# Expert rows weighted at copy-out and summed by accumulating gathers, in a four-layer block on one core

## The reference, cut to what matters

```
logits = x @ w_router                       # 8 experts
top_v, top_i = top_k(logits, 2)
gates = one_hot(top_i) * softmax(top_v)
out = sum over e of gates[:, e] * (silu(x @ w_gate[e]) * (x @ w_up[e])) @ w_down[e]
x = layer_norm(alpha * x + out, g, b)
x = x + (p @ w_ple_proj) * sigmoid(x @ w_ple_gate)
```

## Time and profile before

| what | us |
|---|---|
| median of three runs | 2200.12 (2200.06 to 2201.48) |
| the profiled execution: time | 2201.47 |
| the profiled execution: span | 2199.7 |
| PE busy | 2164.4 |
| DVE busy | 1724.8 |
| ACT busy | 1416.0 |
| POOL busy | 61.7 |

### The profile page before, as it was taken

One profiled execution on the slowest core, in us unless ns is written; L12 is line 12 of the kernel. 1 busy time (PEld: TensorE's weight loads), 2 busy tenths in 40 slices (PEclk: granted clock), 3 DMA queues, 4 the chain that ended last, 5 costly groups with the idle time before them and its releaser, 6 DMA issues.

```text
span 2199.7 us, 30807 instructions
## 1 busy us (share of the span) xinstructions
PE 2164.4 (98%) x11360; PEld 1806.4 (82%) x11360; DVE 1724.8 (78%) x1976; ACT 1416.0 (64%) x1582; POOL 61.7 (3%) x96
## 2 busy tenths in 40 slices
PE   8999999999999999999999999999999999999998
PEld 6788897778888888888888887779978898988888
DVE  6766556688898888888888889767668886776887
ACT  6644444767777777777777777656566556565554
POOL 3000000020000000000000003000000000000000
PEclk9999999999999999999999999999999999999999
DMA  9755554369999999999999999843135554224451
GB/s 390 273 185 190 192 190 175 120 256 397 358 397 368 390 374 384 378 382 380 371 388 376 389 365 403 323 177 130 68 145 190 184 200 148 86 106 157 188 189 61
DMA packets 83523, 573.26 MB, mean 261 GB/s; under 512 B 9744, under 2 KB 10368, under 8 KB 18224
## 3 DMA queue, kind: packets, MB, share of 16 engines
q1 hardware_dynamic: 77760, 545.29, 65.0%
q0 software_dynamic: 5376, 26.12, 3.2%
q10 hardware_dynamic: 288, 0.52, 0.1%
HBM read 564.03 MB, written 17.83 MB: 265 GB/s over the span
## 4 chain that ended last, share of the span: by engine, by line
PE 87%; DVE 6%; ACT 4%; issue 2%; DMA 1%; SPq 0%; POOL 0%; DVEq 0%; ACTq 0%; POOLq 0%
PE bank L829 64%; PE bank L897 10%; PE bank L899 5%; DVE w_lo L540 1%; ACT w_hi L535 1%; PE bank L1188 1%; DVE arena L2411 1%; PE bank L1316 1%; PE bank L1326 1%; ACT arena L1533 1%; DMA raw<-in_wu_qkv 1%; PE bank L952 0%; DVE arena L2091 0%; PE bank L944 0%; PE bank L798 0%
## 5 line engine op out<-in xcount | busy, mean ns | idle before, releaser
L540 DVE TENSOR_TENSOR w_lo<-raw,w_hi 128x2048 fp32r<-128x2048 f32 x505 | 1156.1, 2300 | 249.4 <-ACT w_hi L535 247.7
L535 ACT CAST w_hi<-raw 128x2048 fp32r<-128x2048 f32 x505 | 964.4, 1912 | 357.5 <-PE bank L829 275.1
L829 PE MATMUL bank<-w_hi,xT 128*128 128x512 f32 x2368 | 751.5, 392 | 6.4 <-DVE w_lo L540 3.3
L829 PEld LDWEIGHTS bank<-w_hi,xT 128*128 128x128 f32 x2368 | 444.6, 188 | 107.6 <-issue 7.0
L829 PE MATMUL bank<-w_lo,xT 128*128 128x512 f32 x1184 | 461.0, 389 | 0.0
L829 PE MATMUL bank<-w_hi,aT_hi 128*128 128x512 f32 x864 | 344.4, 399 | 1.0 <-DVE w_lo L540 1.0
L897 PE MATMUL bank<-xT,w_hi 128*128 128x512 f32 x960 | 339.9, 398 | 1.2 <-DVE xT L2035 0.6
L829 PE MATMUL bank<-w_hi,aT_lo 128*128 128x512 f32 x864 | 337.3, 390 | 0.0
L829 PE MATMUL bank<-w_lo,aT_hi 128*128 128x512 f32 x864 | 336.7, 390 | 0.0
L899 PE MATMUL bank<-xT,w_lo 128*128 128x256 f32 x960 | 269.3, 281 | 0.0
L829 PEld LDWEIGHTS bank<-w_lo,xT 128*128 128x128 f32 x1184 | 222.5, 188 | 44.7 <-issue 0.5
(11 more groups left out here) (348 smaller groups left out, 1689.2 us busy)
## 6 DMA issues: line engine op xcount, KB each, us to landing
raw<-in_wu_eg SPq DMA_DIRECT2D x112, 1024.0 KB, 7.3
raw<-in_wu_eu SPq DMA_DIRECT2D x112, 1024.0 KB, 7.2
raw<-in_wu_ed SPq DMA_DIRECT2D x112, 1024.0 KB, 7.2
raw<-in_wu_up SPq DMA_DIRECT2D x44, 1024.0 KB, 4.8
raw<-in_wu_ffn_gu SPq DMA_DIRECT2D x28, 1024.0 KB, 4.8
raw<-in_wu_in SPq DMA_DIRECT2D x28, 1024.0 KB, 4.8
raw<-in_wu_down SPq DMA_DIRECT2D x22, 1024.0 KB, 4.8
raw<-in_wu_ffn_d SPq DMA_DIRECT2D x14, 1024.0 KB, 4.8
```

The costliest lines, as they stand in the source:

```text
L535: nc.scalar.copy(w_hi[:, place(i), :], src).then_inc(*E.hi.mark("unit", i))
L540: nc.vector.tensor_tensor(w_lo[:, place(i), :], raw[:, i % RAW, :], w_hi[:, place(i), :].bitcast(F32), ALU.subtract) \
L829: mm = nc.tensor.matmul(o, l[i], r[j], start=(first and n == 0), stop=(last and n == 2), skip_group_check=not lone)
```

## The change

1. **Weights at copy-out.** Each expert row is scaled when ACT copies it out of its bank. For this DVE computes for each token the slot of its weight, POOL scatters the 512 weights into a DRAM table (four indirect DMAs of one float per partition) and loads it back as `w_slot`; in each turn DVE copies one column to `w_now`, and ACT's copy becomes an activation with a per-partition scale, behind one more wait.
2. **Accumulating gathers.** POOL's product and sum are gone. After the seventh expert's rows are stored, four indirect DMAs with an adding write go straight into R: both tiles for the first choice, then both for the second, each behind its tile's first one. Tokens of the eighth expert are pointed at row 0, which holds zeros.
3. **The eighth expert by a product.** Its rows are never stored. A 0/1 matrix of its members is made ahead of the loop (two DVE compares, two PE transposes, an ACT copy), and behind the loop four float32 matmuls `back x ye` put its rows in token order into banks 0 to 3, from which DVE's `take_rows` adds them. SP no longer waits for gathers.
4. **The branch.** PE's skip over the overflow loop becomes an explicit branch with a prefetch hint that is marked at the top of each turn.
5. **Orders.** One half of the second embedding pair runs behind the transposes of tile 0 in place of two idle products of 256 columns; the zeroing of `ye` moves from DVE (just ahead of the loop) to POOL (behind the norm of the mixer); `rows_and_gates` has fewer dependent steps.
6. **Room.** A constant `which` of 8 columns is added, and the constants' buffer is rounded up from 898 to 928 columns.

```
@@ -239,7 +240,7 @@
-        cst = sb("cst", [P, NC])
+        cst = sb("cst", [P, -(-NC // 32) * 32])
@@ sync: overflow_loads and the unit loads @@
-                    sp.wait_ge(*M.free[1].at("moe", "ye", 1))
-                    sp.dma_start(yg[NE * S:NE * S + P, :], moe["ye"]).then_inc(*M.put.mark("last"))
                     overflow_loads()
-                    for t in range(NT):
-                        sp.wait_ge(*high_in[t].at(t))
@@ gpsimd @@
+            def weights():
+                gp.wait_ge(*y_rows_ready.at())
+                for k, w in enumerate((w1, w2)):
+                    for t in range(NT):
+                        gp.indirect_dma_start(wg, bass.IndirectOffsetOnAxis(ap=w_rows[:, 2 * t + k:2 * t + k + 1], axis=0),
+                                              w[:, t:t + 1], None).then_inc(*wg_put.mark("all"))
+                gp.wait_ge(*wg_put.at("all"))
+                gp.dma_start(moe["w_slot"], wg.rearrange("(h r e) o -> r h (e o)", r=P, e=NE)).then_inc(*w_in.mark())
             def collect():
...
-                for t in range(NT):
-                    fetch(0, t, low_in)
-                gp.wait_ge(*low_in.last())
                 gp.wait_ge(*M.act.at("scaled"))
-                for t in range(NT):
-                    y = moe["y"][:, 0, t, :]
-                    nc.gpsimd.tensor_scalar(y, y, wlo[:, t:t + 1], None, ALU.mult).then_inc(*low_scaled.mark(t))
-                for t in range(NT):
-                    gp.wait_ge(*low_scaled.at(t))
-                    nc.gpsimd.tensor_tensor(R[:, t, :], R[:, t, :], moe["y"][:, 0, t, :], ALU.add).then_inc(*low_added.mark(t))
-                gp.wait_ge(*M.put.at("last"))
-                for t in range(NT):
-                    fetch(1, t, high_in[t])
+                for k in range(2):
+                    for t in range(NT):
+                        if k:
+                            gp.wait_ge(*rows_in[t].at(0))
+                        gp.indirect_dma_start(R[:, t, :], None, yg,
+                                              bass.IndirectOffsetOnAxis(ap=y_rows[:, 2 * t + k:2 * t + k + 1], axis=0),
+                                              compute_op=ALU.add).then_inc(*rows_in[t].mark(k))
+            gp.wait_ge(*x_ready.at(1, "mix", 1))
+            nc.gpsimd.memset(moe["ye"], 0.0).then_inc(*zeroed.mark())
             dispatch()
+            weights()
@@ tensor @@
+            def last_rows():
+                pe.wait_ge(*M.free[1].at("last", "members"))
+                for t in range(NT):
+                    for nb in range(2):
+                        pe.wait_ge(*M.free[nb].at("moe", "ye", nb))
+                        o = open_bank(M, 2 * t + nb)
+                        nc.tensor.matmul(o[:, :], moe["back"][:, t, :], moe["ye"][:, nb * 512:(nb + 1) * 512], start=True, stop=True) \
+                            .then_inc(*M.groups.mark("last", "rows", t, nb))
                 embeddings(L, 0)
                 if L:
-                    embeddings(L, 1)
-                    idle_products(3, 512, 512)
+                    embeddings(L, 1, (0,))
+                    idle_products(0, 512, 512)
                 turn_tile(stage, 0, ready, half=(lambda t: x_half.at(L, "ffn", t)) if L else None)
-                if L == 0:
-                    embeddings(L, 1)
-                else:
-                    idle_products(3, 256, 256)
+                embeddings(L, 1, (1,) if L else range(NT))
...
-                    idle_products(7, 512, 512)
+                    idle_products(7, 512)
+                    last_members()
+                    idle_products(7, 512)
...
                     with pe.Fori(0, NE) as e:
+                        overflow_skip = pe.mark_branch_hint_location()
                         with ev.loop(e):
                             experts(M, "moe", expert_base)
-                    with pe.If(r > 0):
+                    pe.br_lt(r, 1, on_true="pe_past_overflow", on_false="pe_overflow").branch_hint(overflow_skip)
+                    with nc.body("pe_overflow", valid_engines=[mybir.EngineType.PE]):
...
+                    nc.switch_bb("pe_past_overflow")
+                    last_rows()
@@ scalar @@
+                ac.wait_ge(*E.dve.at(tag, "weight"))
                 for h in range(2):
-                    nc.scalar.copy(moe["ye"][:, h * 512:(h + 1) * 512], bank[h][:, :]).then_inc(*E.free[h].mark(tag, "ye", h))
+                    nc.scalar.activation(results[E][:, h * 512:(h + 1) * 512], bank[h][:, :], ACT.Identity, scale=w_now[:, 0:1]) \
+                        .then_inc(*E.free[h].mark(tag, "ye", h))
...
+                    ac.wait_ge(*M.groups.at("last", "members"))
+                    nc.scalar.copy(moe["back"].rearrange("p t n -> p (t n)"), bank[1][:, 0:NT * P]) \
+                        .then_inc(*M.free[1].mark("last", "members"))
@@ vector @@
+                    if f == 1:
+                        ve.wait_ge(*w_in.at())
+                        ve.wait_ge(*turn_before(E.free[1], tag, "ye", 1))
+                        step(V_.tensor_copy(w_now, moe["w_slot"][:, tile:tile + 1, e]), E, tag, "weight")
                     rest_h(f)
...
-                    step(V_.memset(moe["ye"], 0.0), M, "moe", "zeroed")
...
                     def take_rows(t, nb, total):
-                        ve.wait_ge(*high_in[t].at(t))
-                        ve.wait_ge(*low_added.at(t))
+                        ve.wait_ge(*rows_in[t].at(1))
+                        ve.wait_ge(*M.groups.at("last", "rows", t, nb))
                         cols = slice(nb * 512, (nb + 1) * 512)
-                        chain(V_.scalar_tensor_tensor(R[:, t, cols], moe["y"][:, 1, t, cols], whi[:, t:t + 1], R[:, t, cols],
-                                                      ALU.mult, ALU.add, accum_out=total))
+                        V_.scalar_tensor_tensor(R[:, t, cols], bank[2 * t + nb][:, :], 1.0, R[:, t, cols],
+                                                ALU.mult, ALU.add, accum_out=total).then_inc(*M.free[2 * t + nb].mark("last", "rows", t, nb))
```

More of the change, by code:

```diff
@@ L345, in build_program @@
         hot, hot2 = sm(NT, 2, NE), sm(NT, 2, NE)
-        top2, row2, ends = sm(NT, 2), sm(NT, 2), sm(2, NT)
-        w1, w2, swap, wlo, whi = sm(NT), sm(NT), sm(NT), sm(NT), sm(NT)
+        top2, row2, roww, keep = sm(NT, 2), sm(NT, 2), sm(NT, 2), sm(NT, 2)
+        hotw = sm(NT, 2, NE)
+        w1, w2, w_now = sm(NT), sm(NT), sm(1)
         memb, posx = sm(NT, NE), sm(NT, NE)
@@ L571, in overflow_loads @@
                 with sp.If(r > 0):
-                    sp.wait_ge(*M.put.at("last"))
-                    sp.dma_start(yg_own[0, P:S, :], moe["ye"]).then_inc(*V.put.mark("first"))
+                    sp.wait_ge(*M.groups.at("moe", "next", "ga", 1))
+                    sp.dma_start(yg_own[0, P:S, :], moe["xt"]).then_inc(*V.put.mark("first"))
                     for i in range(after, after + RAW):
@@ L1152, in gathered, with last_members @@
                     pe.wait_ge(*E.free[2 + g].at(tag, which, "xe", g))
+            def last_members():
+                pe.wait_ge(*chosen.at())
+                o = open_bank(M, 1)
+                for t in range(NT):
+                    mm = nc.tensor.transpose(o[:, t * P:(t + 1) * P], moe["last"][:, t, :], ident)
+                mm.then_inc(*M.groups.mark("last", "members"))
+            def last_rows():
+                pe.wait_ge(*M.free[1].at("last", "members"))
+                for t in range(NT):
+                    for nb in range(2):
[3 more added lines that the diff above has]
+                            .then_inc(*M.groups.mark("last", "rows", t, nb))
             def turn_tokens():
@@ L1381, in turn_outputs, with embeddings @@
                     mm.then_inc(*M.groups.mark("oT", L, t))
-            def embeddings(L, nb):
+            def embeddings(L, nb, tiles=range(NT)):
                 u = wait_loaded(M, pe, unit_at["pp", L])
                 pe.wait_ge(*params.at("pT", L))
-                for t in range(NT):
+                for t in tiles:
                     o = open_bank(M, 4 + 2 * nb + t)
@@ L2354, in rest_x @@
                 for g in range(2):
+                    if g and which == "first":
+                        select_last()
                     ve.wait_ge(*E.groups.at(tag, which, "ga", g))
```

61 lines of the change are left out of this document (35 added, 26 removed).

## The result

The changed kernel takes **2229.11 us** (2226.94 to 2232.32, four runs) against 2200.3 (2200.06 to 2201.48, four runs) of the kernel before: ratio 1.0129, 95% interval 1.0115 to 1.0143. It is slower by 28.8 us; I had predicted 2196.4, with 2204.5 as the upper end. The profiled execution took 2229.09 us with a span of 2227.3.

The account below looks back on a forecast made before the run. PE, busy 2164.4 of 2199.7 us, was taken as the bound. Tail -3.2, turn eight -2.7, gathers +0.5, copies +1.4 and ahead of the loop +0.3 made -3.7: 2196.4 us against 2200.12, range 2193.5 to 2204.5.

Parts of the forecast that it names:

- The larger constants' buffer: Ahead of the loop: the larger buffer, with the 8 KB fill, adds no work on the path, costed at nothing.
- The gathers: Turn eight: four accumulating gathers replace two plain ones, priced like plain ones at +0.5 us, ends 0 and 16.5.
- rival B: Turn eight: an accumulating gather costs twice a plain one, the weight stream loses 3.3 us, 2199.2 in all; chance 0.16.
- Turn eight: Eighth turn of the expert loop: without POOL's arithmetic DVE splits at 2.29 us again, -2.70 us.
- The scaled copy: ACT's copies at each turn's end: per-partition scale adds 0.2 us per pair, seven turns, +1.4 us, bounds 0 and 2.1.
- The tail: Behind the loop: store and last gather go, PE reaches the transposes earlier and sets the gain; -3.2 us in the sum.
- PE's own part: Behind the loop: PE starts about 0.8 us after the last matmul, keeps its clock, twelve matmuls take 10.4 us.
- DVE's leave of the loop: Behind the loop: DVE skips its overflow branch in ACT's 0.92 us, bounds 0 and 2.98; first sum 3.4 us earlier.
- Ahead of the loop: Before the expert loop: two PE transposes between idle products cost +0.3 us, range 0 to 0.6.
- Rivals D and E: D: hint fails, tail +0.75 us, 2200.4, chance 0.10. E: mark exposes loop's back branch in seven turns, 2217, chance 0.04.

Follow-up runs that it names:

- e1: The kernel before with only the constants' buffer enlarged from 890 to 928 columns, moving everything behind it 128 bytes: 2226.49 us, ratio 1.0116.
- e2: The changed kernel with a constants' buffer of 960 columns in place of 928, 256 bytes further than in the kernel before: 2203.41 us, ratio 1.0008.
- e7: The e2 kernel with its four gathers in turn eight plain in place of accumulating: 2200.02 us, ratio to the kernel before 0.9994.
- e11: The e2 kernel with its four accumulating gathers spread over turn eight, some 17 us apart: 2199.69 us, ratio 0.9991.
- e6: The kernel before with 128 unused bytes ahead of w_hi, so stationary and moving operands move together: 2201.46 us, ratio 0.9999.
- e9: The e2 kernel with PE's hinted branch put back to the plain skip of the kernel before: 2207.18 us, ratio 1.0028.
- e12: The e11 kernel with ACT's last w_hi of a turn ahead of its two scaled copies: 2197.66 us, ratio 0.9981.
- e5: Separate test kernel, only groups of 24 matmuls over operand offsets in 32-byte steps: 5.44 to 5.47 us at equal offsets, 5.58 to 5.62 at most others.
- e10: Separate test kernel like e5, with 4-byte steps and shorter moving operands: 24 matmuls 5.44 to 5.49 us at 256 or 512 bytes, 5.73 at 68.
- e3: The changed kernel with the constants' buffer of 898 columns, not rounded up, 32 bytes further than in the kernel before: 2224.92 us, ratio 1.0106.
- e4: The kernel before with 128 unused bytes just ahead of xT, so xT and aT move while X and R stay: 2226.95 us, ratio 1.0116.
- e13: The e12 kernel with last_rows on PE behind the first four embedding matmuls: 2196.97 us, ratio to the kernel before 0.9982.
- e14: The e13 kernel with DVE's skip of the overflow loop made a hinted branch too: 2197.79 us, ratio 0.9984.

## Why the prediction was wrong, point by point

**The step that failed** stands near the end of the part ahead of the loop: "The larger constants' buffer and the fill of 8 KB early on add no work on the path: nothing." It added no work, and it cost 25.0 us (e1) of the 28.8 by which the changed kernel is slower, and of the 32.7 by which the forecast missed. What the runs showed in its place: the buffer moves xT and aT against w_hi and w_lo by 128 bytes modulo 256, and 24 matmuls of 512 columns take 5.58 us in place of 5.47. Of the 25.0 us 21.2 lie in the eight turns of e1's trace: seven times 2.74 (121.38 against 118.64, 5.4 ns for each of 504 matmuls), and 2.0 in the eighth (123.38 against 121.34). None of my rivals had it: all five asked what new instruction or transfer would wait for what, and none what an unchanged instruction would cost at another address. My test for being wrong, "if the turns grow by more than 0.3 us each", was the one that caught it. With the 2.4 us of the gathers, the 0.7 of the copies and the 1.0 of the tail below, the terms make 29.1 of the 32.7 us. By them the kernel would be 25.4 us slower, just inside the interval of the result (25.3 to 31.5).

**The gathers** were mis-sized: +0.5 us forecast, 2.9 in the changed kernel, 3.8 with the faster matmuls of e2. The model (engine time of the gathers less a cushion of 5.5 us) was good: with the k = 2.0 that e2 and e7 show it gives 3.3. That is rival B's price; that the factor comes from two reads no run shows. The rule that I had set beside it is from the Trainium skill ("Collectives: The Full Stack", section on the bandwidth ceiling): the reduce step of a collective reads two sources, where a copy reads one, and runs at about half its rate. By that rule, the trace agrees: 17.5% against 8.7% for the same bytes. I had the right value in hand and took the nearest row in its place.

**Turn eight** was right: with POOL's arithmetic gone and plain gathers it takes 118.97 us, as the other turns (e7), so the 2.70 us did go; the accumulating gathers gave them back.

**The scaled copy** was nearly right, by mechanism and place: +0.2 us a turn forecast from a pair of 256 columns, 0.30 found, 2.1 us in seven turns in place of 1.4. The pair itself grew from 1.07 to 1.26 us.

**The tail** was forecast at -3.2 and gave -2.2. PE's own part was right: it starts 1.02 us behind the loop, keeps its clock, and does its twelve matmuls in 10.5 us, where I had 10.4. That PE would be the later of the two and set the gain was wrong: it stands 0.59 us for DVE. DVE's leave of the loop was the mis-sized term: 0.92 us taken from ACT, 2.2 found between its last split and its first sum (3.2 us of "issue" that begin beside the split). I had its upper bound, 2.98 from PE, which is nearer in kind. Nor is ACT's leave a constant: the same row shows 0.72 us in the changed kernel, 0.98 in e2 and 3.06 in e11. The tail that I compare with has its own scatter: 21.20 us in the kernel before, 21.83 in e6, whose instructions are the same.

**Ahead of the loop** +0.3 lies within what executions scatter. **Rivals D and E** are out: the hint works (e9), and with the mark and without it a turn is 118.90 us (e2, e9).

With the measured terms and the old relative place the sum is -2.2 - 2.7 + 3.8 + 2.1 + 0.3 = +1.3 us; e2 has +1.95 by the medians. So even without the buffer the change wins nothing: what the tail and POOL gave, the gathers and copies took. With 960 columns, spread gathers and the other order of ACT the same change makes -3.7 us (e12). That this is the figure of my sum is chance: its trace shows the 2.7 us of turn eight and no gain in the tail.

## What to carry to other kernels

A buffer's size is part of a change: it moves all that lies behind it, and matmuls whose operands change their place against each other can lose 2% with no instruction changed (5.58 against 5.47 us for 24). Before reading a diff's logic, compare the mean time of one matmul and the pitch of a long run of them in both traces, and hold the operands' distance fixed when a buffer ahead of one of them grows. Here a multiple of 256 bytes was best for the products of 512 columns and not for the pairs with 256, so which distance suits a kernel has to be timed in it. Where queues are saturated, price an accumulating DMA at twice its bytes and spread such transfers over the stretch instead of issuing them in a row.

## What the runs showed of the hardware that I had not expected

- fp32r matmuls of 512 moving columns in a row cost 227 ns each (5.46 us for 24) where stationary and moving operand begin at equal offsets modulo 256 bytes, 230 at 64 bytes, 233 at the other multiples of 32 bytes, and up to 239 off these steps (5.73 us at 68 bytes; e5, e10). With 256 moving columns equal offsets are the slowest, 120 against 117 ns at 32 bytes (e10), and in the kernel the pairs of 512 and 256 columns take 352 ns at the old place and 347 at 32 bytes more (e3).
- An accumulating indirect DMA takes the DMA engines twice as long as a plain one of the same bytes: 10.5 against 5.2 us of all engines for 2.10 MB (e2, e7).
- The hinted branch cuts PE's idle time behind the loop from 4.72 us to the 1.02 that ACT's copies need, and saves its clock; on DVE the same hint changes nothing (3.35 against 3.20 us).
- PE kept its full clock over an idle time of 1.02 us behind the loop and fell to the 1.2 GHz level behind one of 2.67 (e12), 3.96 (e1, e6) and 4.72 us (e9). But in e4 it stood for 3.14 us and kept a granted clock of 1.00 all the same, its sixteen embedding matmuls in 7.10 us where the kernel before needs 8.77: the length of the idle time alone does not decide.
- DVE's way out of the loop, from the end of what it waits for to its first instruction behind the skip, took 4.5 to 5.7 us (e2, e12, e13, e14), and ACT's 0.72 to 3.06: figures that one trace gives for one engine are no constants.
